# TensorE's two layers written out one behind the other, in a two-layer hybrid encoder step on one core

## The reference

```python
def trunk_layer(x, past, lp):
    h = rmsnorm(x, lp['norm1_g'])
    P = h @ lp['w_in']
    P_rw, P_sa, P_ret, P_gate = split_cols(P, (RW_COLS, SA_COLS, RET_COLS, GATE_COLS))
    y_rw, s_rw_new, shift_new = rwkv_mixer(P_rw, shift_rw, s_rw, lp)
    y_sa, k_new, v_new, ik_new = dsa_mixer(P_sa, pos, k_past, v_past, ik_past)
    y_ret, s_ret_new = retention_mixer(P_ret, pos, s_ret)
    gates = jax.nn.sigmoid(P_gate.astype(F32)).astype(x.dtype).reshape(B, L, N_BRANCH, D_MODEL)
    merged = (gates[:, :, 0] * (y_rw @ lp['w_br_rwkv'])
              + gates[:, :, 1] * (y_sa @ lp['w_br_dsa'])
              + gates[:, :, 2] * (y_ret @ lp['w_br_ret']))
    x = x + merged @ lp['w_o']
    h2 = rmsnorm(x, lp['norm2_g'])
    x = x + jnp.square(jax.nn.relu(h2 @ lp['w_up'])) @ lp['w_down']
    ...
for i in range(DEPTH):          # DEPTH = 2
    ...
    xp, new_p = trunk_layer(xp, past_p, lp)
    xs, new_s = trunk_layer(xs, past_s, lp)
```

## Time and profile before

| | |
|---|---|
| median of three runs | 2942.98 us |
| the profiled execution's own time | 2939.28 us |
| its span, from first to last instruction | 2937.5 us |
| TensorE matmul records | 24862, busy 2684.0 us |
| TensorE weight loads | 24862, busy 2458.4 us |
| mean granted TensorE clock | 0.944 of full |

### The profile page before, as it was taken

The page is one execution under the profiler, slowest core; times in us unless marked ns, Lnnn a source line. Parts: engine busy times, 40 slices in busy tenths (PEclk is TensorE's granted clock), DMA queues, the critical chain, the costliest instruction groups (busy, mean ns, idle before and its releaser), DMA issues.

```text
span 2937.5 us, 61433 instructions
## 1 busy us (share of the span) xinstructions
PE 2684.0 (91%) x24862; PEld 2458.4 (84%) x24862; DVE 1309.0 (45%) x2092; ACT 582.1 (20%) x1269; POOL 1034.8 (35%) x596
## 2 busy tenths in 40 slices
PE   7978899689998999999988688995999889999997
PEld 6977688389987989999978677874998789899997
DVE  3245886433337442332242468854334462522332
ACT  2112223422221120110111112233222211200111
POOL 3502233011223545555534032320212245455553
PEclk9979899699998999999999798996999999999999
DMA  4202112111133312222232111111111342222221
GB/s 168 88 29 62 43 58 70 58 40 54 51 130 107 122 60 85 86 79 86 83 109 73 36 55 50 58 68 46 58 48 54 126 140 94 65 86 80 84 86 54
DMA packets 64555, 222.56 MB, mean 76 GB/s; under 512 B 7888, under 2 KB 8656, under 8 KB 63056
## 3 DMA queue, kind: packets, MB, share of 16 engines
q1 hardware_dynamic: 43200, 158.23, 16.8%
q10 hardware_dynamic: 21136, 61.17, 6.0%
HBM read 190.34 MB, written 29.03 MB: 75 GB/s over the span
## 4 chain that ended last, share of the span: by engine, by line
PE 79%; DVE 10%; DVEq 5%; issue 3%; ACT 2%; ACTq 1%; DMA 0%
PE dense L465 62%; PE mix L465 15%; DVEq L1391 5%; DVE region_b L1571 1%; DVE region_b L1625 1%; ACT region_b L962 1%; PE mix L865 1%; DVE region_b L1627 1%; DVE region_a L1410 1%; DVE in_lo L1744 0%; DVE region_b L1684 0%; DVE region_b L1638 0%; DVE x L1606 0%; PE mix L563 0%; DMA x<-in_x 0%
## 5 line engine op out<-in xcount | busy, mean ns | idle before, releaser
L465 PE MATMUL dense<-act_hi,w_hi 128*128 128x288 f32 x3296 | 976.4, 308 | 30.3 <-DVE act_lo L1403 30.2
L449 POOL TENSOR_SCALAR w_hi<-w_raw 128x1024 fp32r<-128x1024 f32 x296 | 313.2, 1058 | 1845.5 <-PE dense L465 1485.0
L465 PE MATMUL dense<-act_lo,w_hi 128*128 128x288 f32 x3296 | 937.2, 297 | 0.0
L465 PE MATMUL dense<-act_hi,w_lo 128*128 128x288 f32 x3296 | 754.5, 296 | 0.0
L452 POOL TENSOR_TENSOR w_lo<-w_raw,w_hi 128x1024 fp32r<-128x1024 f32 x296 | 721.5, 2437 | 24.6
L465 PEld LDWEIGHTS dense<-act_hi,w_hi 128*128 128x128 f32 x3296 | 626.5, 190 | 90.6 <-issue 49.2
L465 PEld LDWEIGHTS dense<-act_lo,w_hi 128*128 128x128 f32 x3296 | 627.8, 190 | 0.0
L465 PEld LDWEIGHTS dense<-act_hi,w_lo 128*128 128x128 f32 x3296 | 549.8, 190 | 0.0
L465 PE MATMUL dense<-in_hi,w_hi 128*128 128x288 f32 x1408 | 398.3, 296 | 23.8 <-DVE y_mix L1753 12.6
L465 PE MATMUL dense<-in_lo,w_hi 128*128 128x288 f32 x1408 | 397.1, 298 | 0.0
L465 PE MATMUL dense<-in_hi,w_lo 128*128 128x288 f32 x1408 | 305.1, 298 | 0.0
(11 more groups left out here) (180 smaller groups left out, 2583.3 us busy)
## 6 DMA issues: line engine op xcount, KB each, us to landing
w_raw<-in_stream SPq DMA_DIRECT2D x296, 512.0 KB, 3.5
y_mix<-gate_scratch ACTq DMA_DIRECT2D x48, 288.0 KB, 3.0
gate_scratch<-region_b ACTq DMA_DIRECT2D x36, 288.0 KB, 2.1
x_scratch<-x ACTq DMA_DIRECT2D x2, 2304.0 KB, 8.8
y_scratch<-y_mix ACTq DMA_DIRECT2D x2, 2304.0 KB, 8.0
x<-x_scratch ACTq DMA_DIRECT2D x2, 2304.0 KB, 9.7
y_mix<-y_scratch ACTq DMA_DIRECT2D x2, 2304.0 KB, 9.1
gate_scratch<-region_a ACTq DMA_DIRECT2D x12, 288.0 KB, 2.1
```

Source lines behind the costliest of these rows:

```text
L449: nc.gpsimd.tensor_scalar(w_hi[:, v, :], w_raw[:, s, :], 1.0, 1.0, ALU.mult, ALU.mult).then_inc(w_high, 1)
L465: return nc.tensor.matmul(out, lhsT, rhs, start=start, stop=stop, skip_group_check=True)
```

## The change

TensorE's program loses its loop over the layers: Python runs the body twice, with `l` a number, and the text of the second layer stands behind that of the first. The MLP's loop inside each layer stays a loop. The programs of the other four engines are the same, word for word. The order and the number of matmuls don't change.

```diff
             pe.wait_ge(in_const, 48)
             sum_squares(0)
-            with pe.Fori(0, DEPTH) as l:
+            for l in range(DEPTH):
 
                 for t in range(N_RET):
                     fresh = (lambda k: pe.wait_ge(act_ready, l * (2 * KT) + k + 1)) if t == 0 else None
```

## The result

The changed kernel takes 2952.25 us (median of 11 runs, 2947.94 to 2960.63), the kernel before 2942.33 us (11 runs, 2933.22 to 2944.28): a ratio of 1.0043, 95% interval 1.0033 to 1.0052. So it is 9.9 us slower; 2949 was forecast, from 2935 to 2960. The profiled execution took 2951.34 us.

The account below looks back on a forecast made before the run. TensorE was taken as the bound, busy 2684.0 of 2937.5 us. Branch 0, register instructions 0, waits' form +1.0 and MLP loop position +8.7 gave +9.7 on 2939.3: 2949 us, range 2935 to 2960.

Parts of the forecast that it names:

- The layer's branch: Between layers: removing the sequencer's 3772 ns branch gives 0, as TensorE's next matmul waits for act_lo anyway.
- The register instructions: TensorE's sequencer: net 30.5 us less work gives 0, hidden by queued matmuls; at most 3.9 us gained.
- Rival D: Sequencer bounds bursts of small matmuls, so half of 30.5 us or more returns: about 2917 us; chance 0.05.
- The waits' form: At 16 places the last wait moves off the matmul into a separate instruction; net +1.0 us, bounds 0 and +1.5.
- The MLP's loop spans eight blocks: First layer's MLP loop touches eight 256-instruction blocks, a ninth fetched ahead, making its three returns slow; +8.7 us.
- Rival B: Only the form of the waits counts, the MLP loop's position costs nothing: 2940 us; chance 0.35.
- The count of 56 instructions ahead: Instructions taken to stand ahead of TensorE's program, fixing block borders; put at some 55 to 57, 56 used.
- What a miss costs: First layer's three MLP returns: branch 3.77 us, TensorE idle 2.1 us each, 6.3 in all, plus 2.4 for half clock.
- the prediction's two rows: TensorE's clock: it fell to half for 3.2 us after 2.00 us idle, and stayed full after 1.86 us.
- Rival C: At each MLP return the next block is also waited for, another 3.77 us: +18.6, 2958 us; chance 0.10.
- about two or more: Expected sign: instruction fetches on queue 8 for each of three returns in the first layer's MLP, none in the second's.
- the 34 instructions: Loop instructions left in the landing block before block 75 is needed, places 19166 to 19200.

Follow-up runs that it names:

- nopassed: swapped with passed() doing nothing, 606 instructions fewer on TensorE's sequencer; 2944.63 us, ratio 1.0010 to the kernel before.
- swapped: straight with the wait for w_split written last in dense_tile; 2940.88 us, ratio 0.9998 to the kernel before.
- pad60: Changed kernel with 60 increments of an unused counter ahead of the program's first wait; 2959.52 us, ratio 1.0073 to the kernel before.
- gap46: Changed kernel with 46 increments of an unused counter behind the first sum of squares; 2951.62 us, one execution.
- before_pad90: Kernel before, its layer loop kept, with 90 increments of an unused counter at the program's start; 2973.79 us, ratio 1.0121 to the kernel before.
- pad100: Changed kernel with 100 increments of an unused counter ahead of the program's first wait; 2948.24 us, ratio 1.0026 to the kernel before.
- gap82: Changed kernel with 82 increments of an unused counter behind the first sum of squares; 2944.47 us, ratio 1.0006 to the kernel before.
- gap35: Changed kernel with 35 increments of an unused counter behind the first sum of squares; 2941.60 us, ratio 1.0010 to the kernel before.
- gap76: Changed kernel with 76 increments of an unused counter behind the first sum of squares; 2966.32 us, ratio 1.0098 to the kernel before.
- gap40: Changed kernel with 40 increments of an unused counter behind the first sum of squares; 2941.47 us, one execution.
- gap100: Changed kernel with 100 increments of an unused counter behind the first sum of squares; 2949.21 us, ratio 1.0023 to the kernel before.
- straight: Changed kernel with the MLP's loop written out too, no loop left on TensorE; 2942.78 us, ratio 1.0007 to the kernel before.

## Why the prediction was right, and where it was off

- **The layer's branch, 0**: right. The first matmul of layer 2 still waits for `act_lo`, and layer 2 begins with the same distance to before as the first MLP ended (+10.52, +10.20); 3.77 us less on the sequencer gave nothing.
- **The register instructions, 0**: right, and shown beyond the change by nopassed, with 606 instructions less and no gain. Rival D (the sequencer as the bound) falls with it.
- **The waits' form, +1.0**: more of TensorE's idle spans end through a separate wait, 62 where there were 53, and fewer through the wait that the matmul carries, 29 where there were 43; that is 9 to 14 of the 16 that the prediction counted. Their 1 us isn't to be seen: ahead of the first MLP the changed kernel is 1.0 us early, not 0.5 us late. It can't be read from that either, since two other things of its size lie in the same stretch, 0.9 us gained in the RWKV part and 2.0 us lost to half clock at 875.1 us. swapped and nopassed found no price for the form. That it costs exactly nothing isn't shown.
- **The MLP's loop spans eight blocks**: right in kind, the first layer's and not the second's, and shown by moving it: pad60 and gap46 bring slow returns into the second layer, before_pad90 into the old kernel, pad100, gap82 and gap35 take them away. Rival B (nothing comes of it) is out.
- **The count of 56 instructions ahead** was wrong, it is 60. The step that failed is that I read it from two fetches at the ends of layers, and took a fetch's absence for a border not reached. For the kernels at hand it changed nothing: with 60, the changed kernel's first loop still spans blocks 74 to 81.
- **What a miss costs, +6.3 for the idle and +2.4 for the clock**: the branch took 3.9 us against the 3.77 assumed, the first idle 1.8 to 2.0 us against 2.1. The clock fell once in three returns: a spell of 3.4 us, in which TensorE had 3.0 us of work, so 1.5 us lost and not 2.4. Which returns it falls behind isn't told by the length of the idle alone: it fell behind 1.83 us and not behind 1.97 us, and in the kernel before behind an idle of 1.74 us at 885.05 us, which the prediction's two rows leave out. Not in the sum: the second idle, 0.43 + 0.79 + 0.68 = 1.9 us. Idle and clock together measured 7.5 + 1.5 = 9.0 us against 8.7.
- **Rival C** was half right. What lies behind the target is gone as well, with nine fetches at each return and not "about two or more", and the next block is waited for. Nine fetches come out whether the miss empties the store or each fetched block pushes out the one that is needed next; no run tells these two apart. But the next block's fetch runs while the landing block is worked off, so it costs 0.4 to 0.8 us here and not 3.77; the 34 instructions that I named as the cover are 30. In gap76, where only 5 are left, it is 2.3 to 2.9 us. C is therefore a matter of where in its block the loop begins.
- **Not foreseen**: of the 12.0 us in the profiled executions, 2.5 us of the second MLP, and the 2.6 us of the first that idle and clock leave over, are a slower pitch of the matmuls (last section), and -2 us lie elsewhere: the RWKV parts 2.6 us shorter, the stage behind them 5.0 us longer by half clock, and the rest some 4.5 us shorter in small steps. The terms of the prediction that hold in the trace are thus 9.0 of 12.0 us. The median came out at +9.9, the sum at +9.7; with errors of this size in the terms, so close an agreement is partly luck.

The page "Advanced Engine Details and Errata" of the Trainium skill gives TensorE's instruction cache, in the section on the ISA cache, as 128 KB in lines of 256 instructions, which is eight lines. The trace agrees in so far as loops of seven blocks stay with an eighth fetched ahead, and those of eight don't with a ninth fetched ahead, while gap40's eight stayed at the two returns without a ninth. The same section's "only 2 cache lines" can't be about TensorE: a loop of seven blocks fetched nothing in three turns.

## What to carry to other kernels

A loop body of nearly the store's size is a matter of position: here 1579 instructions stayed in the store when they touched seven blocks of 256, and were fetched anew at each turn when they touched eight (with only two places in the eighth, at one return of three). So before a large loop is kept, count its blocks in the built program, and count them again when text ahead of it changes, on the same engine. In the trace the sign is a COMPARE_BRANCH of 4 us instead of 0.2 and instruction fetches in a loop that should have none; 35 idle instructions ahead of it, or no loop at all, took the loss away. Less work for a sequencer whose engine has 2 us of work queued gave nothing here.

## What the runs showed that was not expected

**Two pitches in the MLP.** A turn of the MLP without a slow return takes either 101.13 or 101.76 us, from its first matmul to the next turn's, in kernels whose MLP text is the same. It holds through a passage of the MLP and changes between passages: 10 of the 21 passages without a slow return, in the 14 profiles, were slow ones. Windows of 280 us, TensorE always busy and its clock at 1.00, in the kernel before (two), in the changed one, and in gap35 (two):

```profile
1170.00:1450.00 280.00, 280.00 (x2129) 280.00 (x2128) 90.50 (x68) 33.50 (x49) 152.14 (x88) 1.00 0.26 84
2620.00:2900.00 280.00, 280.00 (x2129) 280.00 (x2128) 91.85 (x69) 33.51 (x49) 152.87 (x89) 1.00 0.25 79
```

```profile
2620.00:2900.00 280.00, 280.00 (x2117) 280.00 (x2116) 92.51 (x68) 34.81 (x51) 151.64 (x88) 1.00 0.25 82
```

```profile
1170.00:1450.00 280.00, 280.00 (x2128) 280.00 (x2127) 90.78 (x68) 33.47 (x49) 152.71 (x89) 1.00 0.26 84
2615.00:2895.00 280.00, 280.00 (x2116) 280.00 (x2115) 92.45 (x68) 34.82 (x51) 151.55 (x88) 1.00 0.25 81
```

2129 matmuls are 131.5 ns each, 2117 are 132.3. gap35 has both in one execution. Per passage it is 2.5 us, up to 5 us in an execution, and so a good part of the runs' spread, and of gap35's remaining 0.10%, perhaps; what chooses the pitch stays open.

**Half clock outside of the MLP.** In the stage between the RWKV part and the branch projections the granted clock falls to 0.50 for one spell more in some executions than in others, though the matmuls are the same. In the first layer it is 3.4 us from 875.1 us on in the changed kernel (2.0 us lost, by the starts of the same matmuls at 866 and 890 us), 6.8 us from 881 on in pad100 and gap100 (4.6 and 4.9 us lost), and the kernel before, straight and gap35 have none between 866 and 885 us. In the second layer it is 3.4 us from 2336.0 us on in the changed kernel (3.0 us lost), 3.4 us in gap35 (2.9 us), 6.8 us in nopassed (5.8 us), and the kernel before has none between 2316 and 2343 us. What chooses it isn't shown: each kernel has one profile. Together with the pitches it means that profiles of kernels that differ in nothing but the order of waits can lie 5 us apart, as swapped and straight do, so a small difference is to be read stage by stage.

**An increment of 51 ns starts every 150 ns** on TensorE's sequencer (100 in 15.2 us). A row's duration is not its price there.

**Late fetches outside of loops.** In the kernel before, TensorE stood still in the RWKV part with nothing to wait for, at 2213.57 us:

```profile
2213.57 1.26 PE L465 MATMUL mix<-x,region_b 64*64 64x64 f32 x34 [1.49 <-issue]
```

One instruction fetch began 2.9 us ahead of it, at 2210.7; in layer 1 the same place shows 0.65 us idle, at 761.9. In the changed kernel that stage is 0.9 and 1.7 us shorter, and so it is, by the same 0.9 and 1.7 us, in before_pad90, which differs from the kernel before by position alone. So straight text doesn't seem free of its fetches: a border that falls into a burst of small matmuls cost 0.9 and 1.7 us here. That the fetch is what TensorE waited for is inferred from its time and from the move; no row names it.
